# Dense feed-forward products in a 2x2x2 scheme of seven products, with sums on VectorE

## What is computed

```
D_FF = 2816
...
def swiglu(x, w1, w3, w2):
    return (jax.nn.silu(x @ w1) * (x @ w3)) @ w2
```

```
    for l in range(DEPTH):
        mod = (cond @ w_mod[l] + b_mod[l])[:, None, :]
```

## Time and profile before

| | |
|---|---|
| median of 3 runs | 2258.41 us (2257.16 to 2260.58) |
| the profiled execution | 2261.39 us, its span 2259.6 us |
| TensorE (PE) busy | 2131.1 us, 94% of the span |
| its weight loads (PEld) | 1536.2 us, 68% |
| VectorE (DVE) busy | 658.4 us, 29% |
| ScalarE (ACT) busy | 362.9 us, 16% |
| HBM read | 417.9 MB, 185 GB/s over the span |
| mean granted TensorE clock | 0.974 of 2.4 GHz |

### The profile page before, as it was taken

The page is one execution under the profiler, slowest core; times in us unless marked ns, Lnnn a source line. Parts: engine busy times, 40 slices in busy tenths (PEclk is TensorE's granted clock), DMA queues, the critical chain, the costliest instruction groups (busy, mean ns, idle before and its releaser), DMA issues.

```text
span 2259.6 us, 33976 instructions
## 1 busy us (share of the span) xinstructions
PE 2131.1 (94%) x14688; PEld 1536.2 (68%) x14688; DVE 658.4 (29%) x1635; ACT 362.9 (16%) x861; POOL 83.2 (4%) x180
## 2 busy tenths in 40 slices
PE   8998998999989989997999999899999998999998
PEld 7786775777677877754653554387677767767776
DVE  1415424333324154233000000235334333440001
ACT  1312230100013122301000000133300012330000
POOL 3000000000000000020000000000001020000000
PEclk9999999999999998997999999999999999999999
DMA  8333234588563342426999999852478763324442
GB/s 251 111 95 122 94 122 149 174 278 286 193 176 101 95 140 77 138 61 197 348 314 378 346 341 335 297 172 98 155 240 271 255 213 110 110 95 141 132 157 93
DMA packets 333817, 421.23 MB, mean 186 GB/s; under 512 B 27222, under 2 KB 282148, under 8 KB 333668
## 3 DMA queue, kind: packets, MB, share of 16 engines
q1 hardware_dynamic: 312464, 352.96, 48.4%
q0 software_dynamic: 13408, 50.66, 6.7%
q10 hardware_dynamic: 7796, 15.43, 2.0%
HBM read 417.90 MB, written 1.05 MB: 185 GB/s over the span
## 4 chain that ended last, share of the span: by engine, by line
PE 53%; DVE 3%; ACT 1%; DMA 1%; issue 1%; ACTq 0%; DVEq 0%
PE psum L1251 11%; PE psum L1368 10%; PE psum L1258 8%; PE psum L1269 6%; PE psum L1428 5%; PE psum L1667 2%; PE psum L1883 2%; PE psum L1287 1%; PE psum L1496 1%; PE psum L1357 1%; PE psum L1441 1%; PE psum L1650 1%; PE psum L1625 1%; PE psum L1178 1%; DVE arena L2057 0%
## 5 line engine op out<-in xcount | busy, mean ns | idle before, releaser
L1251 PE MATMUL psum<-xT,ring 128*128 128x256 f32 x3520 | 786.4, 384 | 4.4 <-ACT small L753 2.1
L1251 PEld LDWEIGHTS psum<-xT,ring 128*128 128x128 f32 x3520 | 672.3, 192 | 119.7 <-issue 20.6
L1269 PE MATMUL psum<-ring,arena 128*128 128x512 f32 x528 | 232.5, 593 | 0.0
L1258 PE MATMUL psum<-ring,xT 128*128 128x256 f32 (+2 forms) x960 | 205.4, 373 | 11.8 <-DVE arena L2296 4.4
L1258 PEld LDWEIGHTS psum<-ring,xT 128*128 128x128 f32 x960 | 174.3, 194 | 40.2 <-DVE arena L2296 5.7
L1269 PEld LDWEIGHTS psum<-ring,arena 128*128 128x128 f32 x528 | 100.2, 190 | 114.7 <-issue 112.4
L2068 DVE TENSOR_TENSOR arena<-arena,psum 128x512 f32<-128x512 f32 x33 | 22.7, 687 | 410.8 <-PE psum L1251 235.0
L2057 DVE SCALAR_TENSOR_TENSOR arena<-arena,cond 128x256 f32<-128x256 f32 x336 | 135.0, 478 | 0.0
L1368 PE MATMUL psum<-ring,arena 128*32 128x256 f32 x2304 | 126.8, 379 | 0.7 <-DVE arena L2140 0.7
L662 ACT ACTIVATE arena<-psum 128x512 f32<-128x512 f32 x33 | 19.7, 597 | 578.2 <-PE psum L1251 571.9
L1368 PEld LDWEIGHTS psum<-ring,arena 128*32 128x32 f32 x2304 | 74.6, 110 | 51.3 <-issue 3.4
(11 more groups left out here) (392 smaller groups left out, 1859.6 us busy)
## 6 DMA issues: line engine op xcount, KB each, us to landing
ring<-in_w_in SPq DMA_DIRECT2D x80, 1024.0 KB, 5.3
ring<-in_exp_w SPq DMA_DIRECT2D x312, 256.0 KB, 6.3
arena<-in_w_mod POOLq DMA_DIRECT2D x48, 1024.0 KB, 10.1
ring<-in_ffn_w SPq DMA_DIRECT2D x33, 1024.0 KB, 7.8
arena<-in_exp_w SPq DMA_DIRECT2D x120, 256.0 KB, 7.1
ring<-in_w_gate SPq DMA_DIRECT2D x22, 1024.0 KB, 7.7
ring<-in_w_up SPq DMA_DIRECT2D x22, 1024.0 KB, 10.1
ring<-in_w_down SPq DMA_DIRECT2D x22, 1024.0 KB, 5.1
```

Source lines behind the costliest of these rows:

```text
L1251: ins = pe.matmul(dst, w[:, k * 256 + c0:k * 256 + c0 + m], act_t[:, k, :], start=(k == 0), stop=(k == KT - 1))
L1258: ins = pe.matmul(dst, act_t[:, k, t * P:t * P + P], w[:, k * 256 + c0:k * 256 + c0 + n], start=(k == 0), stop=(k == KT - 1))
L1269: ins = pe.matmul(psum[:, 4 + 2 * t + h, :], gT[:, s % 3, f * 256 + t * P:f * 256 + t * P + P], w2[:, f * D + h * 512:f * D + h * 512 + 51 ...
```

## The change

Tokens, inner dimension and hidden columns are each cut in two: A is the 256 x 1024 block of tokens in blocks of 128 x 512, B is [w1 | w3] of a step in blocks of 512 x 256. The eight block products become seven, each of 4 matmuls with the tokens (or a sum of token blocks) stationary and 256 hidden columns moving (`product`). VectorE makes three sums of weight blocks in buffers and one in place in the ring (`weight_sums`), four sums of token blocks once a part (`token_sums`), and gathers the products (C11, C22, C21 and one without a name). Since the tokens now lie on partitions, the gated rows (`hidden`) are turned by four transposes on TensorE (`turn_hidden`) and copied to gT by ScalarE. Down of step s - 1 still stands at the end of step s.

The modulation is cut into 20 portions, `modulation(l, first, end)`, over 96 positions of two operations each; the fetches on POOL are as before. The rows' sum over partitions is one piece of 24 matmuls ahead of the last step's down product, and the last down products are put in another order. The operations for the angles (VectorE) and the Sine activations (ScalarE) move from behind the second norm's work to the barrier ahead of the output projection's residual.

The core of the diff:

```diff
-        sil = view(2, 512)
-        gT = view(3, 512)
+        gT = view(2, 512)
+        wsum1, wsum2, wsum4 = view(4, UNIT_FF), view(4, UNIT_FF), view(4, UNIT_FF)
+        part, hh, hidden = view(UNIT_FF), view(4, UNIT_FF), view(NT, UNIT_FF)
+        assert top[0] <= 8192
+        xsum = oT[:, 0:8, :].rearrange("p a b -> p (a b)").rearrange("p (i k t) -> p i k t", i=4, k=4)
...
-                for s in range(FFN_STEPS):
-                    act.wait_ge(*ready("pe_job", "h1", *key, s))
-
+                def keep_hidden(s):
+                    act.wait_ge(*ready("pe_job", "turned", *key, s))
                     if s >= 2:
-                        act.wait_ge(*ready("dve", "g", *key, s - 2))
-                    step(act.activation(sil[:, s % 2, :], psum[:, (2 * s) % 4, :], ACT.Silu), "silu", *key, s)
+                        act.wait_ge(*ready("pe_job", "down", *key, s - 2))
+                    step(act.copy(gT[:, s % 2, :], psum[:, FIRST_BANK, :]), "gT", *key, s)
+
+                act.wait_ge(*ready("pe_job", "h1", *key, 0))
+                step(act.activation(hh[:, 0:4:2, :], two(psum[:, 0, :]), ACT.Silu), "silu", *key, 0)
+                for s in range(1, FFN_STEPS):
+                    act.wait_ge(*ready("pe_job", "P1", *key, s))
+                    if s >= 2:
+                        act.wait_ge(*ready("dve", "C11", *key, s - 1))
+                    step(act.copy(part[:], psum[:, FIRST_BANK, 0:UNIT_FF]), "P1", *key, s)
+                    keep_hidden(s - 1)
+                    act.wait_ge(*ready("dve", "C21", *key, s))
+                    step(act.activation(hh[:, 0:4:2, :], hh[:, 0:4:2, :], ACT.Silu), "silu", *key, s)
+                keep_hidden(FFN_STEPS - 1)
...
+            def product(bank, half, a_blk, b_blk):
+
+                dst = psum[:, bank, half * UNIT_FF:half * UNIT_FF + UNIT_FF]
+                for k in range(4):
+                    ins = pe.matmul(dst, a_blk[:, k, :], b_blk[:, k, :], start=(k == 0), stop=(k == 3))
+                return ins
...
                     for i in range(2):
-                        for f in range(2):
-                            for k in range(KT):
-                                ins = pe.matmul(psum[:, i, f * 256 + t * P:f * 256 + t * P + P],
-                                                wt[i][:, k * 256 + f * P:k * 256 + f * P + P],
-                                                xT[:, k, t * P:t * P + P], start=(k == 0), stop=(k == KT - 1))
+                        ins = token_tile(psum[:, i, t * 256:t * 256 + 256], wt[i], 0, 256, t)
...
+            def turn_hidden(key, s):
+
+                pe.wait_ge(*ready("dve", "g", *key, s))
+                if s < FFN_STEPS - 1:
+                    pe.wait_ge(*ready("act", "P1", *key, s + 1))
+                for f in range(2):
+                    for t in range(NT):
+                        o = f * 256 + t * P
+                        ins = pe.transpose(psum[:, FIRST_BANK, o:o + P], hidden[:, t, f * P:f * P + P], ident[:])
+                job(ins, "turned", *key, s)
+
             def dense(key, hand_over):
                 first_step(key, hand_over)
+                a11, a12, a21, a22 = [xT[:, 4 * (i % 2):4 * (i % 2) + 4, P * (i // 2):P * (i // 2) + P]
+                                      for i in range(4)]
                 w2 = unit(key, "w2", 0)
+                last = FFN_STEPS - 1
                 for s in range(1, FFN_STEPS):
-                    for i, (w, what, eng) in enumerate((("w1", "silu", "act"), ("w3", "g", "dve"))):
-                        b = (2 * s + i) % 4
-
-                        if s >= 2:
-                            pe.wait_ge(*ready(eng, what, *key, s - 2))
-                        wt = unit(key, w, s)
-                        for f in range(2):
-                            ins = channel_tile(psum[:, b, f * 256:f * 256 + 256], wt, f * P, P)
-                        job(ins, "h1" if i == 0 else "h3", *key, s)
-                        used(key, w, s)
-                    if s < FFN_STEPS - 1:
-                        down(key, s - 1, w2)
-                        w2 = unit(key, "w2", s)
-                last = FFN_STEPS - 1
+                    w1, w3 = [unit(key, w, s).rearrange("p (k c) -> p k c", k=KT) for w in ("w1", "w3")]
+                    job(product(FIRST_BANK, 0, a11, w1[:, 0:4, :]), "P1", *key, s)
+                    if s >= 2:
+                        pe.wait_ge(*ready("dve", "C11", *key, s - 1))
+                    product(PAIR_BANK, 0, a12, w1[:, 4:8, :])
+                    pe.wait_ge(*ready("dve", "xsums", *key))
+                    pe.wait_ge(*ready("dve", "wsums", key, s))
+                    job(product(PAIR_BANK, 1, xsum[:, 1], wsum2), "P26", *key, s)
+                    used(key, "w1", s)
+                    if s >= 2:
+                        pe.wait_ge(*ready("dve", "C22", *key, s - 1))
+                    else:
+                        pe.wait_ge(*ready("act", "silu", *key, 0))
+                    product(SIDE_BANK, 1, xsum[:, 2], w3[:, 0:4, :])
+                    job(product(SIDE_BANK, 0, xsum[:, 0], wsum1), "P75", *key, s)
+                    turn_hidden(key, s - 1)
+                    job(product(LAST_BANK, 1, a22, wsum4), "P4", *key, s)
+                    job(product(LAST_BANK, 0, xsum[:, 3], w3[:, 4:8, :]), "P34", *key, s)
+                    used(key, "w3", s)
+                    pe.wait_ge(*ready("act", "gT", *key, s - 1))
+                    if s < last:
+                        downed(down(key, s - 1, w2), key, s - 1)
+                    else:
+                        down(key, s - 1, w2, (0,))
+                    w2_old, w2 = w2, unit(key, "w2", s)
+                down(key, last - 1, w2_old, (1,), (0,))
+                turn_hidden(key, last)
                 if key in MOD_HOME:
-                    add_mod(MOD_HOME[key], 0)
-                down(key, last - 1, w2, (0,))
-                w2_last = unit(key, "w2", last)
-                down(key, last, w2_last, (0,))
+                    add_mod(MOD_HOME[key])
+                else:
+                    downed(down(key, last - 1, w2_old, (1,), (1,)), key, last - 1)
+                pe.wait_ge(*ready("act", "gT", *key, last))
+                job(down(key, last, w2, (0,)), "sum", *key)
                 if key in MOD_HOME:
-                    add_mod(MOD_HOME[key], 1)
-                down(key, last - 1, w2, (1,))
-                down(key, last, w2_last, (1,))
+                    downed(down(key, last - 1, w2_old, (1,), (1,)), key, last - 1)
+                downed(down(key, last, w2, (1,)), key, last)
...
-            def modulation(l, j):
-
-                for i in (j, j + 1):
-                    dve.wait_ge(*ready("modw%d" % (i % 3), l, i))
-                for k in range(KT):
+            def modulation(l, first, end):
+
+                for m in range(first, end):
+                    j, k = 2 * (m // KT), m % KT
                     for i in (j, j + 1):
                         w = modw[:, i % 3, k * UNIT:(k + 1) * UNIT]
                         if k == 0:
+                            dve.wait_ge(*ready("modw%d" % (i % 3), l, i))
                             free(dve.tensor_scalar(pmod[:, i, :], w, cond[:, 0:1], None, ALU.mult))
                         else:
                             dve.wait_ge(S.sem("dve"), S.count["dve"] - 1)
...
+            def weight_sums(key, s):
+
+                for w in ("w1", "w3"):
+                    dve.wait_ge(*ready("slot%d" % ring_place[key, w, s], "unit", key, w, s))
+                w1, w3 = [ring[:, ring_place[key, w, s], :].rearrange("p (k c) -> p k c", k=KT) for w in ("w1", "w3")]
+                if s >= 2:
+                    dve.wait_ge(*ready("pe_job", "P75", *key, s - 1))
+                step(dve.tensor_tensor(wsum1[:], w3[:, 0:4, :], w1[:, 0:4, :], ALU.subtract))
+                free(dve.tensor_tensor(w3[:, 0:4, :], w3[:, 4:8, :], w3[:, 0:4, :], ALU.subtract))
+                step(dve.tensor_tensor(wsum2[:], w3[:, 4:8, :], wsum1[:], ALU.subtract))
+                if s >= 2:
+                    dve.wait_ge(*ready("pe_job", "P4", *key, s - 1))
+                free(dve.tensor_tensor(wsum4[:], w1[:, 4:8, :], wsum2[:], ALU.subtract), "wsums", key, s)
+
+            def token_sums(key):
+
+                a11, a12, a21, a22 = [xT[:, 4 * (i % 2):4 * (i % 2) + 4, P * (i // 2):P * (i // 2) + P]
+                                      for i in range(4)]
+                if key[0] == "ffn1":
+                    dve.wait_ge(*ready("act", "xt", "f1", 0, 1))
+                else:
+                    dve.wait_ge(*ready("act", "modulated", "ffn", key[1], 1))
+                    dve.wait_ge(*ready("dve", "modulated", "ffn", key[1], 1))
+                step(dve.tensor_tensor(xsum[:, 0], a21, a22, ALU.add))
+                free(dve.tensor_tensor(xsum[:, 2], a11, a21, ALU.subtract))
+                step(dve.tensor_tensor(xsum[:, 1], xsum[:, 0], a11, ALU.subtract))
```

(64 more changed lines are left out.)

50 lines of the change are left out of this document (26 added, 24 removed).

## The result

| | before | changed |
|---|---|---|
| median | 2259.49 us (4 runs, 2257.16 to 2260.7) | 2287.16 us (4 runs, 2282.6 to 2291.63) |
| ratio | | 1.0124, 95% interval 1.0098 to 1.0149 |
| profiled execution, its span | 2261.39, 2259.6 us | 2290.09, 2288.4 us |
| mean granted TensorE clock | 0.974 | 0.962 |

A forecast was written before the change was run, and what follows sets the result against it. TensorE bounds the kernel before; VectorE, waiting for exposed fetches, would end last in two parts. Two parts at +25, one at -13 and -1 at part ends gave +36 to +37, 2295 us, range 2258 to 2330.

The forecast's parts named there:

- TensorE, a step: -1.27 us: Dense feed-forward steps: fewer product instructions save 1.73 us, four turns add 0.46, giving a step of 19.41 us.
- the third part: The feed-forward part without modulation: TensorE stays the bound, nothing waits, steps of 19.4 us, -13 us.
- the first step: First step of each feed-forward part: its second token tile goes from 7.25 to 6.91 us, -0.3 us.
- VectorE, 153 us of work: VectorE in a part with modulation, first gating to last: gathering, weight sums and modulation together, against TensorE's 194 us.
- One exposed fetch in each of nine steps, 68 us a part: Modulation-weight fetches waited for in steps 1 to 9: four at 6.3 us, five at 8.9, less 1.5.
- The stretch, 229 us: Ten steps to the last gating's end, with modulation: work, fetch waits and 8 us other waits; 25 us longer than before.
- The tail, 13.6 us: Last gating to last down instruction: turn, 48 row products and 20 down instructions; 18.1 us before, so -4.5.
- Clock, +4 a part: Parts with modulation: about five TensorE idle stretches lower its clock, 1.7 us lost each, half on the path.
- TensorE waits of 30 to 40 us a part: Sign of being right: TensorE waits this long for the gating at the turn in parts with modulation.
- Two lengths of step, near 19.4 and near 28: Sign of being right: steps in parts with modulation have these two lengths, mean 22 to 24 us.
- The waits are covered: Rival: TensorE stays the bound in all three parts, 3 x -13 = -39, 2219 us; chance 0.11.
- The fetches slower yet: Rival: modulation fetches slow because VectorE no longer rests, +10 us a part, 2315 us or over 2330; chance 0.07.

The follow-up runs named there:

- e3: The changed kernel with one of its seven products (P4) computed twice in each step: 2315.32 us, ratio 1.0251 to the kernel before.
- e5: The changed kernel with a fourth modulation-weight slot and the ring loading w2 of step s-1 behind w1 and w3 of step s: 2212.70 us, ratio 0.9801.
- e4: The kernel before, with only its modulation recut into ten equal portions behind the gating: 2249.51 us, ratio 0.9963.
- e7: The changed kernel with TensorE's waits in the two parts with modulation filled by matmuls that nobody reads: 2282.21 us, ratio 1.0109.
- e1: The changed kernel with a fourth slot for modulation weights, so both units of the next pair are fetched early: 2229.06 us, ratio 0.9869.
- e8: The changed kernel, three slots, with modulation in whole pairs behind the gating and ring loads in slot-release order: 2211.12 us, ratio 0.9820.
- e2: The changed kernel with modulation cut as in the kernel before, whole pairs behind the gating, three slots: 2246.22 us, ratio 0.9948.

## Why the prediction was right, and where its sum was off

*TensorE, a step: -1.27 us.* Right: 19.39 us, the third part -12.5 for -13, of which 0.3 were for the first step and lie outside this measure. By the kernels a step has ten waits on TensorE in all, where it had six; the prediction counted ten new ones, at a price of nothing. They cost nothing that shows; e3 and e5 say the same (204.0 us against 216.8 in e4, -12.8 a part where nothing waits in either).

*VectorE, 153 us of work.* A little high: from the first gating to the last VectorE was busy for 147.7 us, 149.6 with the short gaps between dependent operations. The operations took 1.22 to 1.23 us at 1024 columns, and e5, in which TensorE never waits, shows that this work fits beside TensorE's 194 us.

*One exposed fetch in each of nine steps, 68 us a part.* Right in number, and in each of the steps that it named; the sum of 68.4 us agrees because two errors cancel. Forecast were 6.3 us for the four ahead of the gating and 8.9 for the five behind it. Measured were 8.3 in the mean ahead of it (7.41, 9.60, 6.07, 9.98) and 7.1 behind it (9.09, 5.63, 7.01, 7.83, 5.75), the other way round. In the second part, with 64.3 us in all, it is 7.7 and 6.7. Two of them, one behind a gating and one ahead of one:

```profile
516.31 0.35 DVE L2100 TENSOR_SCALAR arena<-arena,cond 128x256 f32<-128x256 f32 x1 [5.63 <-DMA arena<-in_w_mod]
...
581.29 0.35 DVE L2100 TENSOR_SCALAR arena<-arena,cond 128x256 f32<-128x256 f32 x1 [9.98 <-DMA arena<-in_w_mod]
```

What orders them is the distance to the step's turn, as the prediction said; but VectorE was late, and so a fetch ahead of the gating could fall right on the turn. The four fetches released between 0.7 us before and 5 us behind a turn cost 7.4 to 10.0 us, the five released 6 to 10 us behind one cost 5.6 to 7.8.

*The stretch, 229 us.* Measured 227.4, so +23.7 where the prediction had +25. VectorE's other waits, for which I had allowed 8 us, were 9.2, and its work was 3 us less than forecast.

*The tail, 13.6 us.* Measured 14.0, or 14.3 to the very end of the last down instruction, as the prediction counts it. But its price for the row products came from the earlier trace rows, a row behind a 3.05 us wait, and thus at the lower clock; at the full one the tail is 11.9 (e7).

*Clock, +4 a part: this is the term that failed.* It was added on top of a stretch that was itself VectorE's time, and of a tail priced from a slow row. e7 gives 0.6 us in the stretch and 2.1 in the tail (in the second part none and 2.5), and these were already inside the other terms. Without it the sum reads 2 x 20.5 - 13 - 1 = +27, measured +27.7. That this is so close is in part luck, since the fetches, the work and the other waits were each off by some microseconds and cancel. In the traces the second part cost 1.9 us more than the first, because before it had been shorter by 2.9 us with the same work: less of the wait at the row sums, and none of the lower clock.

*TensorE waits of 30 to 40 us a part:* 28.0 us, a little under. *Two lengths of step, near 19.4 and near 28:* the long ones were 24.8 to 30.7.

*The rivals.* "The waits are covered" is what e1, e5 and e8 make true by other means, and their 2211 to 2229 us stand around its 2219. "The fetches slower yet" did not come: landing was 8.2 us in the median of the changed kernel. Where VectorE never stands for a fetch it was 9.6 in e1, which keeps the ring's burst, and 8.8 in the first part of e5, against 10.1 in the earlier trace rows. The Trainium skill's rule (SBUF — State Buffer, "SBUF: two separate sides", VectorE blocking transfers issued from GpSimd) shows no price that could be told apart in any run here; which of VectorE's operations here are in the mode that the rule speaks of, no run here tells.

## What to carry to other kernels

When a change takes slack from an engine, look up every wait that the slack was hiding: here exposed fetches, of which the kernel before could bear 11 a part at no cost (e4), took back more than the whole saving with 9. A buffer is as deep as the moment of its release allows, so place the waiting instruction far behind the releasing one, by another slot or another cut, and queue loads in the order in which their slots come free. And charge the lower clock only where TensorE itself ends last, and not on top of rows that were measured at that level.

## What the runs showed of the hardware

Two queues do not share the DMA engines evenly by bytes: with both busy, in 12 us of e1, POOL's fetches (3.9 KB a packet) moved 2.99 MB while the ring (1.0 KB a packet) moved 1.17. And the time outside the parts, in code that is nearly the same, ranged from 1595 to 1606 us between these traces, one execution of each kernel. It goes with the granted clock there: the 1.2 GHz level was granted outside the parts for 96 to 103 us in the traces of e2, e4 and e8 (1595 to 1596 us), and for 111 to 123 us in the seven others (1600 to 1606 us). Executions of one kernel differ as much: beside e5 the kernel before took from 2249.4 us, at a mean clock of 0.979, to 2264.2 us, at 0.973. What sets the clock there is open, and differences under some 10 us between single traces were therefore read within the parts.
